# Second MoE layer: the number of the fullest expert is handed to the weight-load queue before the full order of experts

## The chip, the cores and the metric

One Trainium2 chip, one core of it. The metric is the device time of one execution in microseconds (us); lower is better. The engines are PE (TensorE, matmuls), DVE (VectorE), ACT (ScalarE), POOL (GpSimd) and SP (SyncE, which here does nothing but issue DMAs). They run side by side and wait for each other by semaphores.

## The reference

A trunk of two layers on 16 meta tokens and 256 input tokens, model width 1024. Layer 1 mixes with a Conformer convolution, layer 2 with differential attention; each is followed by a mixture of experts, with a LayerNorm after every part. The meta tokens are cut off at the end.

```
g_w, g_idx = lax.top_k(softmax(x2d @ w_group + b_group), 1)      # 1 of 4 groups
e_w, e_idx = lax.top_k(softmax(expert logits of that group), 2)  # 2 of its 4 experts
combine = one_hot(g_idx * 4 + e_idx) * (g_w * e_w / sum(e_w))
for each of the 16 experts e:                                    # w1, w3: 1024 x 512, w2: 512 x 1024
    out += combine[:, e] * ((silu(x @ w1[e]) * (x @ w3[e])) @ w2[e])
```

All is float32, so one expert's weights are 6 MB. Which experts have tokens is known only once the router has run.

## The kernel before, in words

**Items.** The tokens that chose an expert are cut into items of up to 32 tokens (`SLOTS`). Only experts with at least one item are computed, and their weights are loaded only then. The work is a list of items, ordered by expert; an expert's place in the order is its turn.

**The order of experts.** VectorE works it out in `post_and_route` after the router's logits. `nit` holds the number of items of each of the 16 experts, and `key` (L1252) is 16 times that number less the expert's number, so that no two keys are equal. A 16x16 comparison of the keys (L1256) and its row sums (L1261) give each expert's rank, and the lines up to L1271 turn rank into turn: the expert with the largest key has turn 0, the one with the smallest live key turn 1, then the others alternate. From the turns two tables are written as integers to `tab`: where each turn's items begin (L1290, semaphore `tab_ready`) and, 16 numbers later, which expert has which turn (L1296, semaphore `order_ready`). After them come the positions of tokens in the list of items, and `pick_item` (L1336 to L1341), which makes the first 0/1 matrix that picks an item's tokens. Each step of this chain on VectorE waits for the one before through one semaphore (`step`, `begin`, `after`).

**Loading weights.** The weights pass through `ring`, 9 bricks of 2 MB; an expert takes 3 (w1, w3, w2), each loaded as two halves of 1 MB. `expert` on SP issues the six halves in the order w1 first half, w3 first half, w1 second, w3 second, w2 first, w2 second. Four transfers are in flight: before each issue SP waits (L301's operands) until the half four places earlier has landed. `experts` runs over the turns. In layer 1 (`FIXED[0]` is 3) the first three turns are experts 0 to 2 whatever the counts are, and are loaded early; in layer 2 (`FIXED[1]` is 0) nothing is loaded before the order is there. So in layer 2 SP waits for `tab_ready` and `order_ready` (L366, L367; the profile shows the wait at L355, the wait for the projection that it was joined with), reads the expert's number with a register load (`nth_expert`, L370), and issues turns 0 and 1, then turn 2 if it has items. `later` does turns 3 to 15; it waits until PE has finished with the brick that is to be overwritten (L342).

**Computing an item.** PE's `mixture` runs 8 keep-warm matmuls (L520), waits for `tab_ready`, gathers the first item's tokens with the pick matrix (L627), and transposes them (L638). Then it reads the turns' first items from `tab` (L283, from the loop at L695) and enters `item` (from L652): 32 matmuls (64 records in the profile) of the gathered tokens with w1 and w3 (L655), four of eight 128-row pieces from the first halves of the bricks and then, after another wait, four from the second halves; the gather of the next item (L627); transposes of the gated result; 16 matmuls (32 records) with w2 (L676), the first half of them with w2's first half-brick. ACT does silu and moves results out, VectorE multiplies and copies. ACT also issues two DMAs with the rows of the last LayerNorm (L1108) ahead of layer 2's mixture.

Of the kernel before, what the change touches and what calls it, by code (L numbers as in the profile page):

```python
# [22 lines left out]
I32 = mybir.dt.int32  # L23
U32 = mybir.dt.uint32
ALU = mybir.AluOpType
ACT = mybir.ActivationFunctionType
AX = mybir.AxisListType.X

P = 128
# [13 lines left out]
EXPERTS = GROUPS * PER_GROUP  # L43
# [16 lines left out]
FIXED = [AHEAD, 0]  # L60
# [73 lines left out]
def trunk(nc, a, out):  # L134
    with ExitStack() as ctx:
        def sb(name, shape, dt=F32):
            return ctx.enter_context(nc.sbuf_tensor(name, shape, dt))
# [3 lines left out]
        def sem(name):  # L141
            if name not in sems:
                sems[name] = ctx.enter_context(nc.semaphore(name))
            return sems[name]
# [8 lines left out]
        tok = sb("tok", [P, 3, D])  # L153
        xT = sb("xT", [P, NC_, T0])
        work = sb("work", [P, 7104])
        small = sb("small", [P, 672])

        tab = sb("tab", [1, 2, ORDER + EXPERTS], I32)
        qswp = sb("qswp", [P, SEQ])
        pos_i = sb("pos_i", [P, 2, 6], I32)  # L160
        ps = ctx.enter_context(nc.psum_tensor("ps", [P, 8, 512], F32))
# [2 lines left out]
        def cst(name):  # L164
            lo, hi = CONST_AT[name]
            return const[:, lo:hi]
# [57 lines left out]
        o_ = 0  # L224

        def sm(n, *dims):
            nonlocal o_
            v = small[:, o_:o_ + n]
            o_ += n
            if len(dims) == 2:  # L230
                v = v.rearrange("p (a b) -> p a b", b=dims[1])
            if len(dims) == 3:
                v = v.rearrange("p (a b c) -> p a b c", b=dims[1], c=dims[2])
            return v
# [15 lines left out]
        lam2, lame, nlam, subg = sm(2), sm(2), sm(1), sm(1)  # L250
        mx, den, rden, r2 = sm(4, 2, 2), sm(4, 2, 2), sm(4, 2, 2), sm(2)
        alpha_b = sm(8)
        assert o_ <= 672
        lgT = view(544, 3 * P)
        PROD, PROD2, PROD3, PROD4 = 1000, 1300, 1600, 1900

# [38 lines left out]
        def _(sp):  # L295
# [39 lines left out]
            def expert(l, b, e, waits, it=0):  # L335


                for i, (m, half) in enumerate(HALVES):
                    if half == 0:
                        waits[m]()  # L340
                    m_before, half_before = EARLIER[i]
                    sp.wait_ge(*arrived(b + m_before, half_before, it))  # L342
                    w = a[("moe_w1", "moe_w3", "moe_w2")[m]]
                    src = w[l, e] if isinstance(e, int) else w[l, bass.ds(e, 1)].rearrange("o r n -> (o r) n")
                    load_half(b + m, half, NC_ if m < 2 else 4, src.rearrange("(k p) n -> p k n", p=P))
# [11 lines left out]
            nothing = lambda: None  # L357

            def experts(l, first_waits):

                b = START[l]
                for e in range(FIXED[l]):
                    expert(l, b + 3 * e, e, first_waits[3 * e:3 * e + 3])
                sp.wait_ge(sem("tab_ready"), l + 1)  # L366
                sp.wait_ge(sem("order_ready"), l + 1)  # L367

                def nth_expert(turn):
                    return sp.value_load(tab[0:1, l, bass.ds(turn + ORDER, 1)], min_val=FIXED[l], max_val=EXPERTS - 1)  # L370

                if not FIXED[l]:
                    first_waits[0]()
                    for turn in range(2):
                        expert(l, b + 3 * turn, nth_expert(turn), [nothing] * 3)
                    lo, hi = first_items(sp, l, 2, 2)
                    with sp.If(hi - lo):
                        expert(l, b + 6, nth_expert(2), [nothing] * 3)
                    with sp.Else():
                        skip(b + 6, 0)  # L380

                def later(bb, turn, it=0):
                    n, _, lo, hi = first_items(sp, l, turn - (AHEAD - 1), 4)
                    w13 = lambda: sp.wait_ge(sem(f"h_ready{l}"), n + 1)
                    w2 = lambda: sp.wait_ge(sem(f"y_ready{l}"), n + 1)
                    with sp.If(hi - lo):
                        expert(l, bb, nth_expert(turn), [w13, nothing, w2], it)
                    with sp.Else():
                        skip(bb, it)

                with sp.Fori(0, 4) as it:
                    for k in range(3):
                        later(b + RING + 3 * k, it * 3 + (k + AHEAD), it)
                later(b + RING * 5, EXPERTS - 1)
# [718 lines left out]
        def _(dve):  # L1113
            steps = [0]

            def step(ins):

                steps[0] += 1
                ins.then_inc(sem("dve_step"), 1)
                dve.wait_ge(sem("dve_step"), steps[0])  # L1120

            def begin(ins):

                steps[0] += 1
                ins.then_inc(sem("dve_step"), 1)
                return steps[0]

            def after(count):
                dve.wait_ge(sem("dve_step"), count)
# [69 lines left out]
            def post_and_route(l):  # L1199
# [37 lines left out]
                if fixed:  # L1237
# [15 lines left out]
                made_live16 = begin(dve.tensor_scalar(live_, nit[:, fixed:], 0.0, None, ALU.is_gt))  # L1253
                later, above = key[:, fixed:], prod4(PROD, (1, rest, rest))[:, 0]
                after(made_key)
                made_above = begin(dve.tensor_tensor(above, later.unsqueeze(1).broadcast_to([P, rest, rest]),  # L1256
                                                     later.unsqueeze(2).broadcast_to([P, rest, rest]), ALU.is_gt))
                after(made_live16)
# [265 lines left out]
```

## Time and profile before

| | us |
|---|---|
| median of 3 runs | 807.36 |
| the 3 runs | 812.84, 807.19, 807.36 |
| the profiled execution, its own time | 812.94 |
| its span, first to last instruction | 810.5 |
| PE busy | 698.3 (86%) |
| DVE busy | 300.6 (37%) |
| ACT busy | 217.9 (27%) |
| weights moved on SP's queue | 157.36 MB, 52.6% of the DMA engines' span |

The span is what the profile shows; the execution's own time is 2.4 us longer. All rows are from this one execution, whose time is 5.6 us above the median of the three runs. Times in rows are microseconds from the span's start. A matmul in float32 appears as two records. In a timeline row the columns are start, duration, engine, line, operation, output<-inputs, sizes and number of instructions merged; in square brackets how long the engine was idle before, and what ended that.

### The profile page before, as it was taken

The page shows a single profiled execution, that of the slowest core. Times are in us where ns is not written, and L with a number is a line of the kernel's source. Part 1 is how long each engine was busy: PE and PEld are TensorE (multiplying, and loading weights), DVE is VectorE, ACT ScalarE, POOL GpSimd, SP SyncE. Part 2 cuts the span into 40 slices and gives each one's busy share as a digit, 9 for nine tenths or more (in the row PEclk, how much of TensorE's full clock was granted, in tenths as well). Part 3 has the DMA queues.
Part 4 walks back from the last instruction along what each step waited for, and adds up shares of the span by engine and source line. Part 5 has one row for each costly group of instructions (what it writes and reads, how often), then busy time and mean ns, then how long its engine had stood idle before and what let it go on. Part 6 is the DMA issues. An engine that isn't in the chain of part 4 may idle for free.

```text
span 810.5 us, 18972 instructions
## 1 busy us (share of the span) xinstructions
PE 698.3 (86%) x7522; PEld 448.3 (55%) x7523; DVE 300.6 (37%) x900; ACT 217.9 (27%) x566; POOL 20.2 (2%) x38
## 2 busy tenths in 40 slices
PE   5998989869989899896479999959976999998864
PEld 4886558536555565452168457747742555554431
DVE  0799731461212222120444017862253222222115
ACT  1641350431212212120331014663140222122130
POOL 0000000000000000000200001100000000000000
PEclk9999999999999999996769999999987999999996
DMA  9999024206799899995599000020017977918804
GB/s 298 365 392 357 9 104 156 105 0 242 278 404 358 305 360 389 357 355 202 177 388 381 2 1 2 1 105 0 1 52 288 398 280 261 378 36 330 323 23 152
DMA packets 86896, 174.54 MB, mean 215 GB/s; under 512 B 7856, under 2 KB 22041, under 8 KB 86857
## 3 DMA queue, kind: packets, MB, share of 16 engines
q1 hardware_dynamic: 72912, 157.36, 52.6%
q10 hardware_dynamic: 11673, 8.13, 3.2%
q0 software_dynamic: 2272, 8.52, 2.9%
q8 instruction: 26, 0.43, 0.2%
q14 instruction: 13, 0.11, 0.0%
HBM read 162.99 MB, written 11.01 MB: 215 GB/s over the span
## 4 chain that ended last, share of the span: by engine, by line
PE 65%; DMA 13%; DVE 9%; ACT 5%; issue 4%; ACTq 2%; SPq 0%; POOL 0%; DVEq 0%; POOLq 0%
PE ps L655 17%; DMA ring<-in_moe_w 11%; PE ps L676 8%; PE ps L493 7%; PE ps L582 4%; PE ps L554 4%; PE ps L565 4%; PE ps L763 3%; PE ps L782 3%; PE ps L627 3%; PE ps L638 2%; PE ps L527 2%; DVE work L1357 1%; PE ps L512 1%; ACT work L975 1%
## 5 line engine op out<-in xcount | busy, mean ns | idle before, releaser
L655 PE MATMUL ps<-ring,work 128*32 128x256 f32 x2816 | 174.1, 401 | 27.9 <-DMA ring<-in_moe_w 14.2
L655 PEld LDWEIGHTS ps<-ring,work 128*32 128x32 f32 x2816 | 106.1, 115 | 88.3 <-issue 42.7
L872 ACT ACTIVATE work<-ps 128x256 f32<-128x256 f32 (+4 forms) x160 | 55.5, 363 | 232.6 <-PE ps L676 95.1
L1357 DVE TENSOR_TENSOR work<-work,ps 64x256 f32<-64x256 f32 x44 | 18.7, 425 | 220.9 <-ACT work L975 220.9
L676 PE MATMUL ps<-ring,work 128*32 128x256 f32 x1408 | 89.8, 383 | 0.0
L627 PE MATMUL ps<-tok,work 128*32 128x256 f32 x928 | 65.6, 389 | 0.0
L1157 DVE SCALAR_TENSOR_TENSOR work<-work,wdw 128x272 f32<-128x272 f32 x150 | 65.2, 500 | 1.0
L493 PE MATMUL ps<-xT,ring 128*128 128x272 f32 x256 | 60.7, 400 | 0.3 <-DVE xT L1134 0.3
L676 PEld LDWEIGHTS ps<-ring,work 128*32 128x32 f32 x1408 | 38.9, 109 | 32.9 <-DVE work L1359 10.2
L493 PEld LDWEIGHTS ps<-xT,ring 128*128 128x128 f32 x256 | 49.6, 194 | 10.8 <-DVE xT L1134 0.4
L975 ACT ACTIVATE work<-ps 64x256 f32<-64x256 f32 x44 | 16.5, 375 | 130.7 <-PE ps L655 130.7
L627 PEld LDWEIGHTS ps<-tok,work 128*32 128x32 f32 x928 | 31.3, 112 | 16.8 <-issue 3.1
L1347 DVE COPY work<-ps 128x256 f32<-128x256 f32 x46 | 19.6, 426 | 45.5 <-PE ps L638 45.5
L582 PE MATMUL ps<-xT,ring 128*128 128x272 f32 x128 | 32.4, 419 | 2.7 <-ACT xT L1025 2.7
L520 PE MATMUL ps<-const 128*128 128x512 f32 x64 | 32.8, 667 | 0.0
L975 ACT ACT_TABLE_LOAD x21 | 26.9, 1283 | 20.9 <-issue 20.8
L782 PE MATMUL ps<-xT,ring 128*128 128x256 f32 x128 | 30.3, 383 | 1.4 <-ACT work L872 1.1
L582 PEld LDWEIGHTS ps<-xT,ring 128*128 128x128 f32 x128 | 26.1, 205 | 8.7 <-ACT xT L1025 2.8
L554 PE MATMUL ps<-work,ring 128*128 128x272 f32 (+1 forms) x128 | 29.0, 387 | 1.4 <-ACT work L1098 0.9
L565 PE MATMUL ps<-work,ring 128*128 128x272 f32 (+1 forms) x128 | 29.5, 386 | 0.0
L554 PEld LDWEIGHTS ps<-work,ring 128*128 128x128 f32 x128 | 24.2, 190 | 6.5 <-ACT work L943 1.3
L763 PE MATMUL ps<-ring,xT 128*128 128x512 f32 x64 | 27.6, 592 | 0.0
(218 smaller groups left out, 699.5 us busy)
## 6 DMA issues: line engine op xcount, KB each, us to landing
ring<-in_moe_w SPq DMA_DIRECT2D x120, 1024.0 KB, 11.8
ring<-in_conv_w_pw SPq DMA_DIRECT2D x12, 1024.0 KB, 11.9
ybuf<-work ACTq DMA_DIRECT2D x44, 128.0 KB
ybuf<-const POOLq DMA_DIRECT2D x2, 2048.0 KB, 7.1
ring<-in_kv_w_k SPq DMA_DIRECT2D x4, 1024.0 KB, 9.3
ring<-in_kv_w_v SPq DMA_DIRECT2D x4, 1024.0 KB, 10.8
ring<-in_attn_w_q SPq DMA_DIRECT2D x4, 1024.0 KB, 10.8
ring<-in_attn_w_o SPq DMA_DIRECT2D x4, 1024.0 KB, 11.4
```

The costliest lines, as they stand in the source:

```text
L493: last = pe.matmul(ps[:, 2 * (c % 2) + s, 0:T0], w[:, k, s, (c % 2) * P:(c % 2 + 1) * P], xT[:, k, :], start=(k == 0), stop=(k == NC_ - 1))
L554: last = pe.matmul(ps[:, c, 0:T], w[:, k, c * P:(c + 1) * P], src[:, k, 0:T], start=(k == 0), stop=(k == NC_ - 1))
L565: last = pe.matmul(ps[:, m_bank(c), 0:T], w[:, k, (c - 4) * P:(c - 3) * P], src[:, k, 0:T], start=(k == 0), stop=(k == NC_ - 1))
L582: last = pe.matmul(ps[:, n % banks, 0:T], w[:, k, (c % 4) * P:(c % 4 + 1) * P], src[:, k, lo:lo + T], start=(k == 0), stop=(k == NC_ - 1))
L627: last = pe.matmul(ps[SLOTS * q:SLOTS * (q + 1), 2, 0:256], pick[:, j, :], tok[:, j, q * 256:(q + 1) * 256], start=(j == 0), stop=(j == TI ...
L655: last = pe.matmul(ps[SLOTS * q:SLOTS * (q + 1), 0, 0:256], xTg[:, k, :], w[:, k, (q % 2) * 256:(q % 2 + 1) * 256], start=(k == 0), stop=( ...
L676: last = pe.matmul(ps[SLOTS * q:SLOTS * (q + 1), 1, 0:256], hT[:, k, :], w2[:, k, q * 256:(q + 1) * 256], start=(k == 0), stop=(k == 3), s ...
L763: last = pe.matmul(ps[:, 4 + i, :], xT[:, k, j * P:(j + 1) * P], w[:, k, :], start=(k == 0), stop=(k == NC_ - 1))
L782: last = pe.matmul(ps[:, 1, 0:SEQ], w[:, k, (c % 4) * P:(c % 4 + 1) * P], xT[:, k, META:T0], start=(k == 0), stop=(k == NC_ - 1))
L872: return act.activation(dst, src, ACT.Copy)
L975: act.activation(hs[64:128, :], ps[0:64, 0, 0:256], ACT.Silu).then_inc(sem(f"silu_ready{l}"), 1)
L1157: ins = dve.scalar_tensor_tensor(cv[:, c, :], glu[:, c, k:k + T0], tap(k, c), cv[:, c, :], ALU.mult, ALU.add)
```

## The change

In layer 2 alone VectorE finds the largest key right after the keys are made, turns it into the number of the expert that has it, writes this number to a new one-element tile `biggest_i`, and signals `biggest_ready`. SP waits for that signal, reads the number, and issues the six halves of that expert before it waits for `tab_ready` and `order_ready`. Turn 1 is then issued as before. `small` grows by 32 columns for two new tiles.

```diff
@@ -153,9 +153,10 @@
         tok = sb("tok", [P, 3, D])
         xT = sb("xT", [P, NC_, T0])
         work = sb("work", [P, 7104])
-        small = sb("small", [P, 672])
+        small = sb("small", [P, 704])
 
         tab = sb("tab", [1, 2, ORDER + EXPERTS], I32)
+        biggest_i = sb("biggest_i", [1, 1], I32)
         qswp = sb("qswp", [P, SEQ])
         pos_i = sb("pos_i", [P, 2, 6], I32)
         ps = ctx.enter_context(nc.psum_tensor("ps", [P, 8, 512], F32))
@@ -250,7 +251,8 @@
         lam2, lame, nlam, subg = sm(2), sm(2), sm(1), sm(1)
         mx, den, rden, r2 = sm(4, 2, 2), sm(4, 2, 2), sm(4, 2, 2), sm(2)
         alpha_b = sm(8)
-        assert o_ <= 672
+        big, bige = sm(1), sm(16)
+        assert o_ <= 704
         lgT = view(544, 3 * P)
         PROD, PROD2, PROD3, PROD4 = 1000, 1300, 1600, 1900
 
@@ -363,6 +365,11 @@
                 b = START[l]
                 for e in range(FIXED[l]):
                     expert(l, b + 3 * e, e, first_waits[3 * e:3 * e + 3])
+                if not FIXED[l]:
+                    first_waits[0]()
+                    sp.wait_ge(sem("biggest_ready"), 1)
+                    biggest = sp.value_load(biggest_i[0:1, 0:1], min_val=0, max_val=EXPERTS - 1)
+                    expert(l, b, biggest, [nothing] * 3)
                 sp.wait_ge(sem("tab_ready"), l + 1)
                 sp.wait_ge(sem("order_ready"), l + 1)
 
@@ -370,9 +377,7 @@
                     return sp.value_load(tab[0:1, l, bass.ds(turn + ORDER, 1)], min_val=FIXED[l], max_val=EXPERTS - 1)
 
                 if not FIXED[l]:
-                    first_waits[0]()
-                    for turn in range(2):
-                        expert(l, b + 3 * turn, nth_expert(turn), [nothing] * 3)
+                    expert(l, b + 3, nth_expert(1), [nothing] * 3)
                     lo, hi = first_items(sp, l, 2, 2)
                     with sp.If(hi - lo):
                         expert(l, b + 6, nth_expert(2), [nothing] * 3)
@@ -1253,6 +1258,11 @@
                 made_live16 = begin(dve.tensor_scalar(live_, nit[:, fixed:], 0.0, None, ALU.is_gt))
                 later, above = key[:, fixed:], prod4(PROD, (1, rest, rest))[:, 0]
                 after(made_key)
+                if not fixed:
+                    step(dve.tensor_reduce(big, key, AX, ALU.max))
+                    step(dve.scalar_tensor_tensor(bige, key, big, cst("expert"), ALU.is_equal, ALU.mult))
+                    step(dve.tensor_reduce(big, bige, AX, ALU.add))
+                    dve.tensor_copy(biggest_i[0:1, 0:1], big[0:1, 0:1]).then_inc(sem("biggest_ready"), 1)
                 made_above = begin(dve.tensor_tensor(above, later.unsqueeze(1).broadcast_to([P, rest, rest]),
                                                      later.unsqueeze(2).broadcast_to([P, rest, rest]), ALU.is_gt))
                 after(made_live16)
```

## Rows read from the trace of the kernel before

**Rows 1.** The page, chain that ended last: share of the span by line
```profile
PE ps L655 17%; DMA ring<-in_moe_w 11%; PE ps L676 8%; PE ps L493 7%; PE ps L582 4%; PE ps L554 4%; PE ps L565 4%; PE ps L763 3%; PE ps L782 3%; PE ps L627 3%; PE ps L638 2%; PE ps L527 2%; DVE work L1357 1%; PE ps L512 1%; ACT work L975 1%
```

**Rows 2.** The same chain in order of time, from 600 us: start, us, what
```profile
612.85 13.07 DMA ring<-in_moe_w
```

**Rows 3.** Timeline of VectorE from the sort keys to the first pick
```profile
605.28 0.18 DVE L1252 SCALAR_TENSOR_TENSOR small<-small,const 128x16 f32<-128x16 f32 x1
...
605.49 0.43 DVE L1256 TENSOR_TENSOR work<-small 128x256 f32<-128x256 f32 x1
605.83 0.16 DVE L1259 TENSOR_REDUCE small<-small 128x1 f32<-128x16 f32 x1
...
606.61 0.23 DVE L1265 SCALAR_TENSOR_TENSOR small<-small 128x16 f32<-128x16 f32 x1
...
609.57 0.16 DVE L1290 CAST tab<-small 1x17 int32<-1x17 f32 x1
...
610.30 0.15 DVE L1296 CAST tab<-small 1x16 int32<-1x16 f32 x1
...
611.93 0.23 DVE L1340 TENSOR_TENSOR work<-work 128x64 f32<-128x64 f32 x1
```

**Rows 4.** SP's queue: register loads of expert numbers (min/median/max ns, starts), then its DMA issues
```profile
L370 SPq TENSOR_LOAD <-tab x2: 278/279/280, 610.5 to 620.0; - x2
...
611.26 2.33 SPq L301 DMA_DIRECT2D ring<-in_moe_w  x4
...
616.48 0.37 SPq L301 DMA_DIRECT2D ring<-in_moe_w  x1
...
619.54 0.37 SPq L301 DMA_DIRECT2D ring<-in_moe_w  x1
...
625.94 0.37 SPq L301 DMA_DIRECT2D ring<-in_moe_w  x1
...
628.64 0.37 SPq L301 DMA_DIRECT2D ring<-in_moe_w  x1
...
631.07 0.37 SPq L301 DMA_DIRECT2D ring<-in_moe_w  x1
```

**Rows 5.** Timeline of PE, from the first gather of layer 2 to the first L676
```profile
614.59 1.07 PE L627 MATMUL ps<-tok,work 128*32 128x256 f32 x16
616.22 0.44 PE L638 MATMUL ps<-const,work 128*128 128x128 f32 x2 [0.56 <-ACT work L872]
619.57 2.92 PE L655 MATMUL ps<-ring,work 128*32 128x256 f32 x32 [2.91 <-DMA ring<-in_moe_w]
626.06 3.64 PE L655 MATMUL ps<-ring,work 128*32 128x256 f32 x32 [3.57 <-DMA ring<-in_moe_w]
...
632.03 1.93 PE L676 MATMUL ps<-ring,work 128*32 128x256 f32 x32
```

**Rows 6.** PE's own queue, 616 to 620 us: its load of item bounds, the item's first instructions
```profile
L283 PEldq TENSOR_LOAD <-tab x1: 1006/1006/1006, 616.5 to 616.5; - x1
...
L652 PEldq FUSED_REGOPS  x2: 42/44/47, 619.3 to 619.4; - x2
```

**Rows 7.** Timeline of PE: an item after a pause, in layer 1 and late in layer 2
```profile
182.18 5.35 PE L655 MATMUL ps<-ring,work 128*32 128x256 f32 x64 [2.25 <-issue]
...
766.84 5.35 PE L655 MATMUL ps<-ring,work 128*32 128x256 f32 x64 [2.22 <-issue]
772.00 1.05 PE L627 MATMUL ps<-tok,work 128*32 128x256 f32 x16
...
773.91 1.93 PE L676 MATMUL ps<-ring,work 128*32 128x256 f32 x32
```

**Rows 8.** Busy time by window: us, PE, PEld, DVE, ACT, POOL, clock, DMA share, GB/s
```profile
626.00:629.70 3.70, 3.64 (x36) 2.02 (x40) 0.00 (x0) 0.00 (x0) 0.00 (x0) 0.50 1.02 403
```

**Rows 9.** The same view, shortly after the number of the expert could be ready
```profile
607.60:608.20 0.60, 0.60 (x2) 0.34 (x1) 0.60 (x3) 0.00 (x0) 0.00 (x0) 0.50 0.04 14
```

**Rows 10.** SP's waits from 600 us on: us in total, times, longest
```profile
SPq L342 <- PE ps L655: 42.6, 2, 26.5
```

## The prediction, made before the changed kernel had run

> **What bounds the kernel now.** I read the profile's chain of waits first, since only work on it can move the end. PE's matmuls hold most of it, and weights arriving by DMA stand second among its lines with 11% of the span, so a stall on the expert weights is real money [rows 1]. Read in order of time, the chain has only one long piece of that kind in the second layer: 13.07 us from 612.85 us on, ending when L655 goes on at 626.06 us [rows 2, 5]. This is the first expert's load. From then to the end the chain is PE's, item after item, so whatever the first item gains the rest of the kernel inherits.
>
> Then I followed what starts that load. VectorE makes the sort key at 605.28, writes the table at 609.57 and the order of experts at 610.30, ended 610.45 [rows 3]. SP reads the order at 610.5 and issues its first half-brick at 611.26, which is 0.81 us after the order was written [rows 4]. Four halves are in flight; each later issue waits for an earlier landing, so the issue times are the landing times: the first half of w1 had landed at 616.48, of w3 at 619.54, the second half of w3 at 625.94, and the two halves of w2 at 628.64 and 631.07 [rows 4].
>
> Last I looked at what PE does meanwhile, since a load that comes sooner helps only if PE can use it. It gathers at 614.59, transposes at 616.22, starts the item's L655 at 619.57, stops after 32 of its 64 records, resumes at 626.06 and reaches L676 at 632.03 [rows 5]. The profile puts the start at 619.57 down to the DMA, but the rows of PE's own queue say otherwise: its load of the item bounds begins at 616.5 and takes 1.006 us, and the last two register operations of the item (L652) run at 619.3 and 619.4 [rows 6]. PE came to its wait for weights 0.15 us before it passed. The transfer that really stops PE is the second pair of halves, 622.5 to 626.06.
>
> **The change, part by part.** *Added on VectorE:* a maximum over 16 keys, a compare-and-multiply with that maximum as operand, a sum over 16, and a cast of one element, between the key (605.28) and the 16x16 comparison (605.49). The nearest rows are the short reduce at 605.83 (0.16 us), the operation with a per-partition operand at 606.61 (0.23) and the cast at 609.57 (0.16) [rows 3]. With 0.04 us between steps that depend on each other: 605.49 + 0.16 + 0.04 + 0.23 + 0.04 + 0.16 + 0.04 + 0.16 = 606.32. The comparison follows some 0.08 us before that end, so all that stands behind it moves by about 0.75 us. From both sides: no less than 0.4 us (four starts 0.1 us apart, as the two from 605.28 to 605.49 with an unconnected one between them), no more than four of the longest neighbour, L1256's 0.43, so 1.7 us. I take 0.82 us for the number's readiness, as the rows are of the same sizes.
>
> *What that delay hits:* the table (609.57 to 610.3), the order, the picks (L1340 ends 612.16, to 612.9) [rows 3]. PE waits for the table and the picks only before its gather at 614.59, behind its keep-warm matmuls, so 2.4 us of cover are left before the 0.75 [rows 3, 5]. At 1.7 us the cover still holds. ACT and POOL read the table too, but they wait next for the gather and for the first results, which come far later. Cost: nothing.
>
> *Moved on SP:* the load of a register, and the six DMA issues of the first expert, ahead of the waits for table and order. SP has nothing else in its queue there; its waits on the earlier bricks and on the projection are long met. From number to first issue I take the 0.81 us of before: first issue 606.32 + 0.81 = 607.13, against 611.26, so 4.13 us earlier. The register load may take 0.28 us as in the two rows on SP or 1.01 as PE's [rows 4, 6]; it reads the same kind of word on the same engine, so 0.28. With both upper ends (0.9 us more on VectorE, 0.7 on SP) the lead is 2.5 us, with the lower end 4.5. The wait for the full order that remains sits after the first expert's six issues, the last of which comes at 619.54 - 4.13 = 615.4, when the order (611.2) is long written: it costs nothing. The second expert thus follows in the stream as before.
>
> *What becomes of 4.13 us:* landings at 612.4, 615.4, 621.8 (the pair that counts), 624.5 and 626.9. PE starts the item at 619.45, not 615.5: its queue sets that, and 0.1 us is all it gains there. But now the second pair is there when the first 32 records end, and the item runs through. The trace has two first items that run through after just such a pause of PE, at 182.18 and at 766.84 (idle 2.25 and 2.22 us before): both take 5.35 us for the 64 records, and L627 follows 5.16 us after the start, L676 another 1.91 us later [rows 7]. So L676 begins at 619.45 + 5.16 + 1.91 = 626.5 instead of 632.03. Its weights are there at 624.5, and those of its second half at 626.9, when about 627.5 would want them. The shift is 5.5 us; I take 0.1 off for the second pair, which arrives within 0.1 us of its use: **5.4 us**. That this exceeds the 4.13 us of the load is not an error: before, both halves of the item ran mostly at the low clock (32 records in 3.64 us, granted clock 0.50) because PE stood still between them [rows 5, 8], while 64 together take 5.35.
>
> *Whether the stream's start meets other traffic:* the two layer-norm rows loaded by ACT are nearly through when the first ring packets could come: DMA share 0.04 from 607.6 to 608.2 [rows 9]; the first issue at 607.13 needs about 1 us before bytes flow. The Trainium skill, "DMA: Bandwidth & Descriptors", section "Issuing engines are not separate DMA queues", says that transfers of all issuing engines interleave on the same 16 DMA engines. By that rule an early load would share with them and gain less, by at most that remnant of 0.6 us; by the row the remnant is 4% of it. The sum is the same by both to 0.1 us.
>
> *Afterwards:* SP's longest wait in this layer is 26.5 us for L655 before it may overwrite a brick [rows 10]. The later loads hang on PE, wait that long, and move with it. Nothing gives the gain back.
>
> **The sum** for the profiled execution: span 810.5, time 812.94, less 5.4, gives 807.5. The median shown is 807.36 (807.19 to 812.84), 5.6 below the profiled time. I take the shift over unchanged, since it lies in one stretch: 807.36 - 5.4 = **802.0 us**.
>
> **Rivals.**
> *The clock doesn't come back in the first item.* Then the first 32 records end at 619.45 + 2.92 = 622.37, and from there to L676 it takes what it took, 632.03 - 626.06 = 5.97 us [rows 5]: 628.3, a gain of 3.7, time 803.7. For: it stayed at half through that stretch before [rows 8]. Against: there PE stood still for 3.5 us in it, which it no longer does, and the two rows without a stop recovered [rows 7].
> *The clock never falls in it.* Then the second pair at 621.8 and the second w2 half at 626.9 are late in turn: the second half of L676 (about 633.0 before) begins at 626.9, a gain of 6.1, time 801.3. For: the pause before the item is unchanged at 2.9 us, and a fall may fall elsewhere in another run. Against: both rows of such starts show it, and so does this start itself, whose 32 records took 2.92 us [rows 5, 7]. The Trainium skill, "TensorE: Matmul & The Clock Gate", section "What's actually happening", says that the point of change varies from run to run, as the monitor doesn't start with the kernel; by that rule this rival and the one before each come up in some runs, by the rows in none.
> *The median lands on the upper of the times seen.* The three runs lie 5.65 us apart; if the changed kernel's middle run is like the slowest, 812.84 - 5.4 = 807.4, about no change.
> *Slower: the low clock outlasts the first item.* Place: the items from 632 on. Price: 64 + 32 + 16 records at half speed instead of full, which is 3.5 + 1.8 + 0.9 = 6.2 us for each item (from 3.64 for 32 against 1.93 for 32 [rows 5, 7]). With one such item the gain is gone (803.7 + 6.2 = 809.9), with two it is 816.1. For: the start of the item falls at another moment of the load stream. Against: from 626 on PE has no pause. The added VectorE steps can't do it: they would have to grow beyond 2.4 + 5.4 us.
>
> **How the numbers follow.** Forecast 0.55, clock stays low 0.15, never falls 0.10, upper of the times 0.15, slower 0.05. The cases 801.3 to 803.7 with the unknown lead (2.5 to 4.5 us; at 2.5 the second pair lands 1.6 us later and the gain is 3.8) span 801 to 804; the fourth case reaches 807.4, and it takes in the 0.8 left. Range 800.6 to 807.8. About 1%, 8.1 us, is what a measurement of this kernel can tell from no change. Faster than 799.3 needs more than every case gives: 0.04. Slower than 815.4 only by the last rival with two items: 0.03. Within 1%: 0.93.
>
> **What would show it.** First ring issue of the second layer's experts near 607.1 and about 3.5 us before the order is written; the table 0.75 us later; gather still at 614.6; L655 from 619.45 in one run of 64 records, 5.3 us long; L676 at 626.5; from there every distance as before. I am wrong if L655 still stops in its middle by over 0.5 us, if it starts much before 619.3 (then PE's queue was not the bound), or if the gather moves.

## The result and the profile after

| | before | after |
|---|---|---|
| median of 20 runs each, us | 811.51 (807.19 to 814.78) | 806.10 (801.72 to 809.54) |
| profiled execution, us | 812.94 | 804.83 |
| its span, us | 810.5 | 802.6 |

The ratio is 0.9946, with a 95% interval from 0.9931 to 0.9961: 4.4 us faster (3.2 to 5.6, each as the ratio's distance from 1 times 811.5). The two medians differ by 5.4 us. The change moves the time by half a per cent, and that is clear of noise. Two later comparisons of the same kernel gave 0.9943 (0.9917 to 0.9970) and 0.9933 (0.9906 to 0.9960). The two profiled spans lie 7.9 us apart, which is more than the change gave: 1.0 us of it lies ahead of the keys and 0.9 us behind the last L676 (now L681), where the two kernels do the same; 5.9 us lie in the stretch that is looked at below.

The line numbers have moved: L1252 is L1257 now, L655 is L660, L676 is L681, L627 is L632, L301 is L303. Everything ahead of the keys happens to be 1.04 us earlier in this trace, so I count from the keys: 605.28 in [rows 3], 604.24 here. VectorE's timeline, start and duration:

```profile
604.24 0.18 DVE L1257 SCALAR_TENSOR_TENSOR small<-small,const 128x16 f32<-128x16 f32 x1
...
604.45 0.17 DVE L1262 TENSOR_REDUCE small<-small 128x1 f32<-128x16 f32 x1
604.65 0.23 DVE L1263 SCALAR_TENSOR_TENSOR small<-small,const 128x16 f32<-128x16 f32 x1
604.92 0.17 DVE L1264 TENSOR_REDUCE small<-small 128x1 f32<-128x16 f32 x1
605.12 0.14 DVE L1265 CAST biggest_i<-small 1x1 int32<-1x1 f32 x1
605.20 0.40 DVE L1266 TENSOR_TENSOR work<-small 128x256 f32<-128x256 f32 x1
...
609.99 0.15 DVE L1306 CAST tab<-small 1x16 int32<-1x16 f32 x1
```

The number is ready at 605.26, 1.02 us after the keys begin; the order is written at 610.14, 5.90 us after them, against 5.17 before [rows 3]. The four steps cost the chain 0.73 us. SP's queue, its register load of the new tile first:

```profile
L371 SPq TENSOR_LOAD <-biggest_i x1: 292/292/292, 605.3 to 605.3; - x1
...
606.10 2.32 SPq L303 DMA_DIRECT2D ring<-in_moe_w  x4
...
611.39 0.37 SPq L303 DMA_DIRECT2D ring<-in_moe_w  x1
...
614.35 0.37 SPq L303 DMA_DIRECT2D ring<-in_moe_w  x1
...
620.79 0.37 SPq L303 DMA_DIRECT2D ring<-in_moe_w  x1
...
623.50 0.37 SPq L303 DMA_DIRECT2D ring<-in_moe_w  x1
...
625.92 0.37 SPq L303 DMA_DIRECT2D ring<-in_moe_w  x1
```

From the keys, the first issue comes after 1.86 us (5.98 before), the second pair's landing after 16.55 (20.66), w2's last half after 21.68 (25.79) [rows 4]. All three leads are 4.1 us in this pair of traces. In the two further traces of the changed kernel the second pair landed 16.9 and 16.0 us after the keys, so its lead is 3.7 to 4.6 us. Traffic of other transfers cost the early start next to nothing: the first half-brick landed 5.3 us after its issue, 5.2 before. PE's timeline, to set beside [rows 5]:

```profile
612.78 1.07 PE L632 MATMUL ps<-tok,work 128*32 128x256 f32 x16
614.41 0.44 PE L643 MATMUL ps<-const,work 128*128 128x128 f32 x2 [0.56 <-ACT work L877]
617.55 5.41 PE L660 MATMUL ps<-ring,work 128*32 128x256 f32 x64 [2.69 <-issue]
622.77 1.05 PE L632 MATMUL ps<-tok,work 128*32 128x256 f32 x16
...
624.78 2.24 PE L681 MATMUL ps<-ring,work 128*32 128x256 f32 x32
626.83 3.64 PE L660 MATMUL ps<-ring,work 128*32 128x256 f32 x64
```

The item's 64 records run through in 5.41 us, where before there were two runs of 32 with 3.57 us of standing still between. The idle time before the item, 2.69 us, is now put down to "issue" (PE waited for nothing that the profile shows) and no longer to a DMA, and PE's own queue shows the same steps as in [rows 6]:

```profile
L285 PEldq TENSOR_LOAD <-tab x1: 1003/1003/1003, 614.6 to 614.6; - x1
L657 PEldq FUSED_REGOPS  x2: 42/44/47, 617.3 to 617.4; - x2
```

One thing is new. L681 takes 2.24 us instead of 1.93 [rows 5]: its second half waits for w2's last half, which landed at 625.92. The chain of waits shows the hand-over between load and PE at just that point:

```profile
614.35 11.55 DMA ring<-in_moe_w
625.90 0.04 issue
625.95 1.07 PE ps L681 x16
627.02 3.50 PE ps L660 x64
```

I use one measure in what follows, the **stage**: from the start of the keys to the first matmul of the second item (L655, now L660). Before it took 633.78 - 605.28 = 28.50 us, after 626.83 - 604.24 = 22.59 us. One part of the stage has nothing to do with the change: the keep-warm matmuls ahead of the gather take 8.8 to 9.65 us from trace to trace, by how much of them falls into a stretch at the low clock (granted clock 0.50), and the gather starts 8.1 to 9.3 us after the keys. Where PE and not the load ends the stage, this difference goes straight into it: in experiment 3 and its repetition the gather starts 8.55 and 8.99 us after the keys, and the stage takes 22.24 and 22.77.

### The profile page after: what moved, and what is told of

It reads as the page before. It is cut to its first block, busy times and chain, and to the rows that moved or that the text cites. A ratio compares the mean times of both kernels' runs of the same rounds, so it can differ in the third digit from the quotient of the medians.

```text
span 802.6 us, 18977 instructions
## 1 busy us (share of the span) xinstructions
PE 697.1 (87%) x7522; PEld 447.0 (56%) x7523; DVE 301.2 (38%) x904; ACT 218.2 (27%) x566; POOL 20.5 (3%) x38
## 4 chain that ended last, share of the span: by engine, by line
PE 65%; DMA 14%; DVE 9%; ACT 5%; issue 4%; ACTq 2%; POOL 0%; SPq 0%; POOLq 0%; DVEq 0%
PE ps L660 16%; DMA ring<-in_moe_w 11%; PE ps L681 8%; PE ps L498 7%; PE ps L587 4%; PE ps L559 4%; PE ps L570 4%; PE ps L768 3%; PE ps L787 3%; PE ps L632 2%; PE ps L643 2%; PE ps L532 2%; DVE work L1367 1%; PE ps L517 1%; ACT work L980 1%
## 5 line engine op out<-in xcount | busy, mean ns | idle before, releaser
L660 PE MATMUL ps<-ring,work 128*32 128x256 f32 x2816 | 172.6, 399 | 23.1 <-issue 16.4
L660 PEld LDWEIGHTS ps<-ring,work 128*32 128x32 f32 x2816 | 104.8, 115 | 84.1 <-issue 40.4
L681 PE MATMUL ps<-ring,work 128*32 128x256 f32 x1408 | 90.0, 384 | 0.1
L632 PE MATMUL ps<-tok,work 128*32 128x256 f32 x928 | 64.2, 382 | 0.0
L681 PEld LDWEIGHTS ps<-ring,work 128*32 128x32 f32 x1408 | 38.8, 109 | 33.3 <-DVE work L1369 10.4
L632 PEld LDWEIGHTS ps<-tok,work 128*32 128x32 f32 x928 | 30.3, 109 | 16.1 <-issue 1.5
L1199 DVE TENSOR_TENSOR xT<-xT,ps 128x272 f32<-128x272 f32 (+1 forms) x16 | 6.8, 430 | 56.0 <-PE ps L570 29.5
```

Source lines behind the costliest of these rows:

```text
L632: last = pe.matmul(ps[SLOTS * q:SLOTS * (q + 1), 2, 0:256], pick[:, j, :], tok[:, j, q * 256:(q + 1) * 256], start=(j == 0), stop=(j == TI ...
L660: last = pe.matmul(ps[SLOTS * q:SLOTS * (q + 1), 0, 0:256], xTg[:, k, :], w[:, k, (q % 2) * 256:(q % 2 + 1) * 256], start=(k == 0), stop=( ...
L681: last = pe.matmul(ps[SLOTS * q:SLOTS * (q + 1), 1, 0:256], hT[:, k, :], w2[:, k, q * 256:(q + 1) * 256], start=(k == 0), stop=(k == 3), s ...
```

## The experiments

All edits are to the changed kernel unless said otherwise; "ratio" is that to the kernel before, run beside it on the same chip. Stages are read off each run's trace as above.

**1. The cost alone: the steps stay, SP loads as before.**

```diff
-                if not FIXED[l]:
-                    first_waits[0]()
-                    sp.wait_ge(sem("biggest_ready"), 1)
-                    biggest = sp.value_load(biggest_i[0:1, 0:1], ...)
-                    expert(l, b, biggest, [nothing] * 3)
...
-                    expert(l, b + 3, nth_expert(1), [nothing] * 3)
+                    for turn in range(2):
+                        expert(l, b + 3 * turn, nth_expert(turn), [nothing] * 3)
```

> The four VectorE steps and the tile stay, SP loads as before the change (order first). My theory: the steps move the table and the picks by 0.75 us, all of it inside the 2.4 us of cover before the gather, so the time is that of the kernel before (811.5 median) within 0.5 us, and from the keys to the second item's L655 it takes 28.5 us as before, or 29.2 since SP's own order comes 0.75 us later and this load is on the path: time +0.7. Rival (the steps cost nothing anywhere, the change is pure gain): +0.0. Rival (the steps reach the gather): gather 0.75 us later against the end of the keep-warm matmuls.

Measured: ratio 1.0001 (0.9981 to 1.0021), stage 29.07 us. SP's first issue comes 6.70 us after the keys, 0.72 later than before, the stage is 0.57 us longer than in the first trace of before, and the time doesn't resolve it. So without the early load nothing is gained. That the steps cost something here only because the order stands on the load's path fits the 0.72 us, but one trace doesn't show it. In this trace the gather follows the keep-warm matmuls at once, as before:

```profile
603.55 9.63 PE L522 MATMUL ps<-const 128*128 128x512 f32 x16
613.11 1.07 PE L629 MATMUL ps<-tok,work 128*32 128x256 f32 x16
```

The picks stay hidden behind the keep-warm matmuls.

**2. Part of the lead: the same four steps, moved behind the turns** (behind the last line that writes `turn_of`, nothing else changed).

> The number is worked out from the same keys, but only after the turns are, about 1.4 us later. The lead of the load falls from 4.1 us to about 2.7 us. Theory that the lead passes to PE one to one and the rest is PE's running through: the second pair of halves lands about 18 us after the keys, PE pauses 1 to 1.7 us in the middle of the item, gain over the kernel before 2.7 to 4.4 us. Rival (only PE's own pace counts once the load is somewhat early): the full 5.4 us gain stays.

Measured: ratio 0.9954 (0.9931 to 0.9976), 3.7 us below before; stage 25.41 us, 3.1 less than before's first trace and 2.2 less than its second (experiment 8). The first issue comes 3.55 us after the keys, a lead of 2.4 us. PE's timeline:

```profile
619.47 3.11 PE L660 MATMUL ps<-ring,work 128*32 128x256 f32 x32 [2.80 <-issue]
624.18 3.25 PE L660 MATMUL ps<-ring,work 128*32 128x256 f32 x32 [1.60 <-DMA ring<-in_moe_w]
```

PE stands for 1.60 us in the middle, inside the 1 to 1.7 that the first theory asked for. A full gain at 2.4 of the 4.1 us of lead is excluded for the stage: it would need 22.6 us. (The ratio alone can't be told from that of the changed kernel, 0.9946.) As long as the second pair lands late, the load's lead is what PE is paid by.

**3. All the lead: a constant expert, loaded long before.**

```diff
-                    sp.wait_ge(sem("biggest_ready"), 1)
-                    biggest = sp.value_load(biggest_i[0:1, 0:1], ...)
-                    expert(l, b, biggest, [nothing] * 3)
+                    expert(l, b, 9, [nothing] * 3)
...
-                    step(dve.tensor_reduce(big, key, AX, ALU.max))
-                    step(dve.scalar_tensor_tensor(bige, key, big, cst("expert"), ALU.is_equal, ALU.mult))
-                    step(dve.tensor_reduce(big, bige, AX, ALU.add))
-                    dve.tensor_copy(biggest_i[0:1, 0:1], big[0:1, 0:1]).then_inc(sem("biggest_ready"), 1)
```

> The first expert of layer 2 is a constant (number 9, the fullest for these inputs), its six halves are issued as soon as the bricks are free, some 20 us before the keys, and VectorE's added steps are gone. It measures what is left for the weights to give. Theory (after the change PE's own queue and clock set the first item, the weights only graze it): 0.3 to 0.6 us faster than the changed kernel, L655 starting 3.1 us after the transposes as before, 64 records in 5.3 us. Rival (the weights are still the bound): 2 us or more faster than the changed kernel.

Measured: stage 22.24 us, only 0.35 less than after, with the item's records in one run and L679 at its usual 1.93 us:

```profile
619.83 5.35 PE L658 MATMUL ps<-ring,work 128*32 128x256 f32 x64 [2.71 <-issue]
...
626.99 1.93 PE L679 MATMUL ps<-ring,work 128*32 128x256 f32 x32
```

The six halves are issued from 22.1 us before the keys and have all landed 3.1 us before them, so they lie there for 16 us when the item starts. The ratio, 0.9901 (0.9875 to 0.9926) from 6 runs, spoke for the rival: 3.7 us below the changed kernel. Stage and time disagreed, so both were measured again (runs 12 to 14). By the stage, weights that are there from the start give only a few tenths more; what is left belongs to PE.

**4. PE's clock in the first item.** `loaded_ahead_warm` adds five matmuls behind the first transposes of layer 2:

```diff
                 turn_gathered(l, 0, True)
+                if l == 1:
+                    keep_warm(5, 5)
```

> As loaded_ahead, and five more keep-warm matmuls between the first item's transposes and the item in layer 2, while PE's queue reads its bounds. Theory (the item's 5.3 us instead of 3.6 are the low clock after PE's pause): L655 takes 3.6 us for its 64 records and the time is 1.7 us below loaded_ahead. Rival (the item is slow for another reason, instruction fetch for one): 5.3 us as before, time unchanged.

Measured: ratio 0.9913 (0.9892 to 0.9935), stage 22.53 us. Both halves of it are right and cancel:

```profile
615.79 4.46 PE L523 MATMUL ps<-const 128*128 128x512 f32 x10
620.17 3.66 PE L658 MATMUL ps<-ring,work 128*32 128x256 f32 x64
```

The 64 records take 3.66 us instead of 5.35, so the low clock is the cause of the 1.7 us, and the five matmuls take 4.46 us where PE's queue needs 3.15, which loses 1.5 us again. Between the gather and the second item the stage is 0.16 us shorter than in experiment 3, as 1.7 less 1.5 should give; that the whole stage is 0.3 us longer is the 0.45 us that the keep-warm matmuls ahead of the gather took longer in this trace (9.34 against 8.89). Experiments 5 and 6 use three matmuls. Beside them the changed kernel itself ran again:

> The changed kernel, once more, for a time and a stage beside the three others of this call. The stage from the keys (L1257) to the start of the second item's L660 took 28.50 us before and 22.59 after. Expected again: 22.2 to 23.0 us, and 4 to 5.5 us below the kernel before, over more runs of both.

Measured: ratio 0.9943 (0.9917 to 0.9970), stage 22.97 us. This trace has both late loads, a stop of 0.85 us for the second pair and of 0.22 us for w2:

```profile
614.50 3.26 PE L660 MATMUL ps<-ring,work 128*32 128x256 f32 x32 [2.79 <-issue]
618.61 1.93 PE L660 MATMUL ps<-ring,work 128*32 128x256 f32 x32 [0.85 <-DMA ring<-in_moe_w]
...
623.65 1.07 PE L681 MATMUL ps<-ring,work 128*32 128x256 f32 x16 [0.22 <-DMA ring<-in_moe_w]
```

**5. Three matmuls, with the weights ahead** (`keep_warm(5, 3)` in the kernel of experiment 3).

> As loaded_ahead (constant expert 9, weights there long before), with three keep-warm matmuls instead of five. Theory (low clock after the pause costs 1.7 us, and five matmuls were too many: they ended 1.5 us after PE's queue had reached the item): item starts 3.1 us after the transposes and its 64 records take 3.6 us; stage 20.5 us against 22.24 with no extra matmuls. Rival (the matmuls always delay the item by what they save): stage 22.2 us again.

Measured: stage 20.53 us, as forecast to 0.1; the item starts 3.15 us after the transposes and takes 3.66 us.

```profile
612.63 2.74 PE L523 MATMUL ps<-const 128*128 128x512 f32 x6
615.50 3.66 PE L658 MATMUL ps<-ring,work 128*32 128x256 f32 x64
```

The ratio, 0.9929 (0.9904 to 0.9955), can't be told from that of the changed kernel. With the weights out of the way, PE's low clock is worth 1.7 us of stage.

**6. Three matmuls in the changed kernel.**

> The changed kernel with three keep-warm matmuls (2.6 us) between the first item's transposes and the item in layer 2. Theory (the weights and PE's low clock are nearly equally late after the change): L660 itself speeds up from 5.3 towards 3.6 us where the clock stays up, but stops for the second pair of halves, and L681 stops for the last half of w2, which lands 21.7 us after the keys: the stage stays at 22.5 us, no gain over 0.3 us. Rival (the low clock alone costs the 1.7 us): stage 20.9 us, 1.7 us faster.

Measured: ratio 0.9951 (0.9927 to 0.9975), stage 22.81 us, no gain over 22.59 and 22.97.

```profile
617.51 2.74 PE L525 MATMUL ps<-const 128*128 128x512 f32 x6
620.39 1.93 PE L660 MATMUL ps<-ring,work 128*32 128x256 f32 x32
623.97 1.93 PE L660 MATMUL ps<-ring,work 128*32 128x256 f32 x32 [1.65 <-DMA ring<-in_moe_w]
...
629.01 1.07 PE L681 MATMUL ps<-ring,work 128*32 128x256 f32 x16 [0.22 <-DMA ring<-in_moe_w]
```

PE computes at full clock and stands 1.65 us instead. Against the changed kernel's mean stage of 22.87 us (three traces), weights ahead alone give 0.4 us (22.24 and, repeated, 22.77), the clock alone nothing, both together 2.3: after the change the two are late by nearly the same amount. The differences of a few tenths among these stages are no larger than what the keep-warm matmuls ahead of the gather add or leave out; the 2.3 us are.

**7. A sooner number, with the three matmuls.** The keys are made from the token counts, ahead of the two steps that turn them into item counts, and the four steps for the number follow at once:

```diff
+                if not fixed:
+                    step(dve.scalar_tensor_tensor(key, nit, float(EXPERTS), cst("minus_e"), ALU.mult, ALU.add))
                 if not fixed:
                     step(dve.tensor_reduce(big, key, AX, ALU.max))
...
+                over = prod4(PROD, (1, 16, FULL))[:, 0]
```

> As after_warm3, and in layer 2 the keys are made from the token counts themselves instead of the item counts, so that two VectorE steps (0.31 and 0.30 us) leave the way to the number; the order of experts with the same number of items may differ, the sum does not. Theory (the weights set the stage once the clock is kept): it takes 0.6 us less than after_warm3, measured from the counts' reduce (L1245 of the changed kernel, 0.91 us ahead of its keys): 22.8 us against 23.4. Rival (PE's queue sets it): no difference.

Measured: ratio 0.9920 (0.9896 to 0.9944), stage from the reduce (the sum over the counts that the keys are made from, L1245) 23.51 us against 23.72 in after_warm3. The first issue did come 0.67 us sooner after the reduce (2.09 against 2.76 us), but from it to w2's last landing it took 20.51 us against 20.04. This stretch varies between 19.8 and 20.5 us from trace to trace, more than the step is worth.

**8. The kernel before, again.**

> The kernel before, once more. It gives a second trace of its stage and says what this comparison reads where there is no difference. Expected: ratio 1.000 within 0.2%; from the keys to the second item's L655 between 27.5 and 28.6 us (28.50 in the first trace), the lower end if the clock happens to be up in the item's second half, where 3.64 us for 32 records would be 1.9. Rival (the first trace was typical to 0.2 us, and the times of whole runs differ elsewhere): 28.3 to 28.7.

Measured: ratio 0.9995 (0.9978 to 1.0011), which is what the comparison shows for no difference. Stage 27.64 us:

```profile
618.67 3.64 PE L655 MATMUL ps<-ring,work 128*32 128x256 f32 x32 [5.09 <-DMA ring<-in_moe_w]
624.18 3.31 PE L655 MATMUL ps<-ring,work 128*32 128x256 f32 x32 [1.87 <-DMA ring<-in_moe_w]
627.30 1.05 PE L627 MATMUL ps<-tok,work 128*32 128x256 f32 x16
```

The second pair is used 20.76 us after the keys, as in the first trace (20.78), so the load that stops PE is the same to 0.02 us. The 0.86 us lie behind it: here the clock is back for L627, which takes 1.05 us, and there it was not. The stage of before depends on the clock after the pause, by this much. The start of the item is different too. Here PE waited for it, 5.09 us idle: the first half of w3 landed 15.2 us after the keys (14.2 in the first trace), and the transposes, behind shorter keep-warm matmuls, were 1.2 us sooner after the keys. PE's queue needs some 3.2 us from the transposes to the item, so the load and not the queue set this start, by 2.3 us; in the trace of number_unused, with 3.62 us idle for the DMA, it did so too, by some 0.9.

**9. A sooner number without the matmuls.**

> The changed kernel with keys from the token counts, without extra keep-warm matmuls: the number is ready 0.67 us sooner. Theory (weights and PE's pace are within 1 us of each other): the stage from the counts' reduce takes 23.2 us against 23.5 and 23.88 in the two traces of the changed kernel, 0.3 to 0.6 us less; in time at most 0.7 us, below what the rounds resolve. Rival (weights alone decide): the full 0.67 us; rival (PE alone): nothing.

Measured: ratio 0.9915 (0.9884 to 0.9945), stage from the reduce 23.92 us: nothing of 0.67 us in this trace, and a ratio better than the stage explains. No wait for weights is left in the first item here, and the keep-warm matmuls took 9.64 us, so PE alone set this stage. Repeated below.

**10. PE's queue sooner.** The bounds are read ahead of the gather, and three experts stand outside the loop:

```diff
+                early = first_items(pe, l, 0, 4) if l == 1 else None
                 gather(l, 0, True, range(TILES[l]))
...
+                if l == 1:
+                    for k in range(3):
+                        expert(START[l] + 3 * k, early[k], early[k + 1], 0)
-                with pe.Fori(0, 5) as it:
+                with pe.Fori(l, 5) as it:
```

> The changed kernel; PE reads the first four item bounds of layer 2 ahead of the gather and the first three experts stand outside the loop, so that PE's queue reaches the first item some 1.5 to 2 us sooner after the transposes (3.1 to 3.3 us in all traces so far). Theory (the weights bound the end of the first item once PE is a little earlier): L660 starts sooner, then stops longer for the second pair, stage from the keys 22.5 to 23.0 us, no gain. Rival (PE's queue sets it, as I put it in the prediction): stage 21 us, 1.5 us faster.

Measured: ratio 0.9961 (0.9936 to 0.9986), stage 23.89 us, 1 us longer than without it. The item starts 0.96 us after the transposes instead of 3.1, then:

```profile
618.23 1.93 PE L660 MATMUL ps<-ring,work 128*32 128x256 f32 x32 [0.52 <-DVE work L1361]
...
623.47 2.65 PE L660 MATMUL ps<-ring,work 128*32 128x256 f32 x32 [3.31 <-DMA ring<-in_moe_w]
625.82 2.01 PE L632 MATMUL ps<-tok,work 128*32 128x256 f32 x16
```

It reaches the second pair sooner, stands 3.31 us, and computes what follows at the low clock (L632 at 2.01 us instead of 1.05). In this one trace a head start that ended in a pause was worse than none; the ratio can't be told from that of the changed kernel.

**11. The same with the weights ahead and three matmuls.**

> Constant expert 9 long before, three keep-warm matmuls, and the bounds read ahead: with weights out of the way, what PE's queue alone is worth. Theory: the three matmuls (2.6 us) now hide nothing of the queue but delay the item themselves, so the item starts 2.9 us after the transposes instead of 3.15: stage 20.2 to 20.5 us, next to no gain over ahead_warm3 (20.53). Rival: below 20 us.

Measured: ratio 0.9937 (0.9915 to 0.9958), stage 20.79 us against 20.53. The matmuls fill the time that the queue gave up, as the theory had it; the item starts 2.95 us after the transposes. The stage is 0.3 us above its band because the keep-warm matmuls ahead of the gather took 9.32 us against 8.87 in experiment 5; from the gather on it is 0.2 us shorter, as the item's start is.

**12 to 14. The changed kernel and the two variants for which stage and time disagreed, again, on one chip.**

> The changed kernel a third time, for a third trace of the stage and a time beside the two others of this call. Two traces gave 22.59 and 22.97 us from the keys to the second item against 28.50 and 27.64 before, a gain of 4.7 to 5.9; the two comparisons gave 4.4 and 4.6 us. Expected: stage 22.5 to 23.0, ratio 0.9935 to 0.9955.

> number_from_counts again. Its first comparison gave 0.9915 (0.9884 to 0.9945), 2.5 us below the changed kernel's 0.9946, while its trace shows next to nothing of it in the stage (23.92 us from the reduce against 23.50 and 23.88). Theory (weights and PE equally late, the first ratio was luck): ratio within 0.15% of after_third's. Rival (a real gain outside the stage): again 0.2% or more below it.

> loaded_ahead again. Its first comparison gave 0.9901, 3.7 us below the changed kernel's 0.9946, its stage only 0.35 to 0.7 us less. Theory: ratio 0.9925 to 0.9945, 0.3 to 0.9 us below after_third. Rival (weights that land long before give 2 us or more by another way, which the stage doesn't hold): 0.992 or less again.

| | first ratio | again | stage from the reduce, us (first, again) |
|---|---|---|---|
| changed kernel | 0.9946, 0.9943 | 0.9933 (0.9906 to 0.9960) | 23.50, 23.88; 23.96 |
| number_from_counts | 0.9915 | 0.9932 (0.9910 to 0.9955) | 23.92; 23.25 |
| loaded_ahead | 0.9901 | 0.9946 (0.9919 to 0.9972) | 23.15; 23.67 |

(From the keys, the changed kernel's stages are 22.59, 22.97 and 23.05 us; from the counts' reduce each is 0.91 longer. The third has no wait for weights at all and is the longest, since its keep-warm matmuls took 9.62 us against 8.89 and 8.81; number_from_counts had 9.64 and, again, 8.80.) The advantages of 2.5 and 3.7 us did not repeat: on one chip the three lie within 0.0014 of each other. The first ratios of the two variants came from 6 runs each. No version tried is shown to be faster than the changed kernel; the stage allows 2.3 us for one that has both the weights and the clock, and that one used an expert number known beforehand.

## Why the prediction was right or wrong

*The cost on VectorE.* Forecast 0.82 us (0.83 by its own sum, 606.32 - 605.49) from the comparison's old place to the number, and 0.75 us of delay behind; 0.81 and 0.73 in the trace. Nothing of it reached the gather. Right, with less room than I gave: the 2.4 us between the picks and the gather belong to slow keep-warm matmuls. In before_again there were 1.2 us, and after the change 0.92, 0.47 and 1.66 us were left. The upper end of 1.7 us of delay, which I called harmless, would have reached the gather in after_again, by 0.5 us.

*The lead.* Forecast 4.13 us, measured 4.1 at the first issue, and in the first pair of traces at the second pair and the last half of w2. Right.

*PE's queue sets the item's start, not the weights.* Right for the changed kernel: with the weights lying there for 16 us the item still starts 3.15 us after the transposes, and with the bounds read ahead it starts after 0.96. For the kernel before it is nearly so in the first trace only, where the load came 0.1 us behind PE's queue; in before_again the load set the start, so there the change moved the start too (15.25 us after the keys before, 12.9 to 14.1 after). What I missed is that an earlier start is worth nothing while the second pair lands when it does: experiment 10 let the item start 2.2 us sooner after the transposes, and the stage got longer.

*The item runs through, so the gain exceeds the lead.* Forecast L676's start 5.5 us sooner, with 0.1 off for the second pair. In the first pair of traces it was 6.2 us (from the keys, 26.75 before, 20.54 after), because the keep-warm matmuls ended 0.8 us sooner; that was the clock during them, not the change, since before_again shows 8.81 us for them instead of 9.65. Over the traces the stage is 28.50 and 27.64 before, 22.59, 22.97 and 23.05 after: 5.2 us in the mean, from 4.6 to 5.9. The forecast was 5.4.

*The weights are only just on time.* I gave 0.1 us for the second pair and expected w2's last half 0.6 us ahead of its use. It was late by 0.2 to 0.3 us in two of three traces, and the second pair by 0.85 us in one. A term mis-sized by up to 1 us, towards a smaller gain. The rival of the clock that doesn't come back shows up in part: in after_again it stayed low through the first 32 records (3.26 us) and was back for the rest (1.93 us). The Trainium skill's rule of the prediction, that the point of change varies from run to run ("TensorE: Matmul & The Clock Gate", "What's actually happening"), agrees with that: in the three traces of the changed kernel the granted clock fell to 0.50 at 0.2, 0.4 and 0.9 us after the item's first matmul, and these 64 records took 5.41, 3.26 + 1.93 and 5.35 us. The case of the clock that never falls did not come up in them.

**The step that failed** is the last one, "I take the shift over unchanged ...: 807.36 - 5.4 = 802.0 us". The shift held (4.4 us by the ratio, 5.4 between the medians), the base didn't: 807.36 was the middle of three runs, and that of 20 runs is 811.51. The measured 806.1 lies 4.1 us above 802.0, and 4.15 of base explain it. Against the 811.51 of the 20 runs, 802.0 would be 9.5 us faster, over twice what the ratio shows. That the measured time lies in the stated range is owed to the rival on the upper of the times, not to the sum. The sign was in the text: the profiled execution had 812.94, one of the three runs 812.84, and I gave only 0.15 to the case that the median sits at the upper end. My chances also put 0.93 on "within 1%" and so told nothing of whether the kernel gets faster: 0.54% is within 1% and is a real gain. They rested on about 1% as what can be told from no change; 20 runs of each told 0.15%. The rival on the slower side had no part in the first items; its price of 6.2 us for an item is 6.0 by the rows that it names (3.64 against 1.93 us for 32 records).

## What to carry to other kernels

When a load is started sooner, list what the consumer does in the meantime and which of its waits ends last after the move: here the lead of 4.1 us was paid in full, plus about 1 us in the mean of the stages, which I put down to the clock that the pause in the middle had cost, and then weights, PE's queue and the clock stood within a microsecond of each other, so that no single further fix gave more than a few tenths. When runs of a kernel spread more than the effect, take the base from the profiled execution and the runs together, forecast the difference, and prove it by a stage's length in several traces: the stage repeated to 0.5 us after the change and 0.9 before it, while two ratios with 6 runs each lay 0.17% and 0.45% from their repetition.

## What the runs showed of the hardware that I had not expected

A pause of PE of 2.7 to 2.8 us ahead of the first item was followed by a fall of the granted clock to 0.50 within 1 us of the item's start in all 8 traces that have it and had the first weights ready, and where the weights were there the 64 records took 5.35 us instead of 3.66 (experiments 3 and 5). With three or five matmuls on constants in that pause the clock didn't fall in any of 5 traces; three remove the loss, five cost nearly what they save.

A somewhat shorter pause falls well or badly from trace to trace. At the item with which PE's loop begins its third turn, late in layer 2, 64 records took 5.35 us in this trace of the changed kernel:

```profile
759.91 5.35 PE L660 MATMUL ps<-ring,work 128*32 128x256 f32 x64 [2.20 <-issue]
```

and 3.66 us in that of number_unused, after a pause of the same length:

```profile
765.98 3.66 PE L657 MATMUL ps<-ring,work 128*32 128x256 f32 x64 [2.21 <-issue]
```

From the second item to the last L676 it took 147.1 us in 9 of the 17 traces and 148.5 to 148.8 in the other 8, with nothing between. The 8 are exactly the traces in which this one item took 5.25 to 5.35 us; in the 9 it took 3.66. The pause of 1.5 us ahead of the loop's second turn was followed by 3.66 us in all 15 traces that have it. Differences of this kind in the other stages would add up to the spread of 8 us between runs; that they make all of it wasn't tried.

Six loads of 1 MB, four in flight, take 19.8 to 20.5 us from the first issue to the last landing, for the same expert and the same order; issued 22 us ahead of the keys (experiments 3 to 5, 11 and 14) they took 19.0 to 20.1.
